# Two normalisations of a fused two-layer block: order of the first product's tiles, place of the weight splits, and the modulation sums

## Reference

```python
# block 1
u = rmsnorm(h, norm_mix)                 # first norm
proj = u @ w_in                          # q, k, v of the delta rule first
...
h = h + square(relu(rmsnorm(h, norm_mlp) @ w_up)) @ w_down
gate = sigmoid(rmsnorm(h, norm_ple) @ w_ple_gate)
h = rmsnorm(h + gate * (p @ w_ple_proj), norm_final)
# block 2
mod = silu(c) @ w_ada + b_ada            # 6 x 1024 values: shift, scale, gate, twice
x = rmsnorm(h, norm_mix_2) * (1 + scale) + shift      # second norm
q = x @ w_in_2[:, 0:512]                 # query product of the retention
```

## Time and profile before

| | before |
|---|---|
| median of 3 runs | 2023.18 us |
| the profiled execution's own time | 2023.73 us |
| its span, first to last instruction | 2021.9 us |
| PE busy | 1936.7 us (96%) |
| DVE busy | 1340.7 us (66%) |
| ACT busy | 892.1 us (44%) |
| POOL busy | 505.7 us (25%) |
| mean granted clock of TensorE | 0.983 |

### The profile page before, as it was taken

One profiled execution on the slowest core, in us unless ns is written; L12 is line 12 of the kernel. 1 busy time (PEld: TensorE's weight loads), 2 busy tenths in 40 slices (PEclk: granted clock), 3 DMA queues, 4 the chain that ended last, 5 costly groups with the idle time before them and its releaser, 6 DMA issues. The chain is left out here.

```text
span 2021.9 us, 24041 instructions
## 1 busy us (share of the span) xinstructions
PE 1936.7 (96%) x8921; PEld 1572.1 (78%) x8921; DVE 1340.7 (66%) x1421; ACT 892.1 (44%) x973; POOL 505.7 (25%) x266
## 2 busy tenths in 40 slices
PE   7998999999999999999999999999999999999992
PEld 6877887888888878768887787877887888878872
DVE  5538857666674666434036464757988998989994
ACT  2224324322323451232002213226887888878883
POOL 3520014000000003515664453510221222321122
PEclk8999999999999998999999999999999999999996
DMA  5321102656552231243236162333999999999994
GB/s 174 111 63 63 34 23 95 207 178 198 199 170 99 100 106 46 91 167 104 88 100 249 63 240 72 108 137 124 371 364 376 371 374 380 378 383 358 358 346 156
DMA packets 115307, 385.38 MB, mean 191 GB/s; under 512 B 21845, under 2 KB 24196, under 8 KB 88734
## 3 DMA queue, kind: packets, MB, share of 16 engines
q1 hardware_dynamic: 98800, 349.88, 47.8%
q10 hardware_dynamic: 10382, 25.42, 3.9%
q0 software_dynamic: 6048, 9.03, 1.3%
HBM read 353.49 MB, written 43.79 MB: 196 GB/s over the span
## 5 line engine op out<-in xcount | busy, mean ns | idle before, releaser
L2949 DVE TENSOR_TENSOR m_lo<-m_raw,m_hi 128x2048 fp32r<-128x2048 f32 x200 | 448.7, 2285 | 9.2 <-ACT m_hi L2877 8.6
L2877 ACT ACTIVATE m_hi<-m_raw 128x2048 fp32r<-128x2048 f32 x200 | 382.7, 1921 | 103.7 <-DMA m_raw<-in_w_exp_gate_dram 71.7
L264 PE MATMUL ps<-xhi,whi 128*128 128x512 f32 x936 | 375.8, 401 | 11.1 <-DVE xlo L461 5.9
L266 PE MATMUL ps<-xhi,wlo 128*128 128x512 f32 x936 | 366.5, 392 | 0.0
L265 PE MATMUL ps<-xlo,whi 128*128 128x512 f32 x936 | 366.3, 391 | 0.0
L241 POOL TENSOR_SCALAR whi<-raw 128x2048 fp32r<-128x2048 f32 (+1 forms) x55 | 104.2, 1894 | 851.6 <-PE ps L266 786.5
L243 POOL TENSOR_TENSOR wlo<-raw,whi 128x2048 fp32r<-128x2048 f32 (+1 forms) x55 | 254.5, 4628 | 4.6
L264 PE MATMUL ps<-m_hi,xt_hi 128*128 128x512 f32 x544 | 217.0, 399 | 8.6 <-DVE xt_lo L2954 7.1
L264 PEld LDWEIGHTS ps<-xhi,whi 128*128 128x128 f32 x936 | 177.0, 189 | 53.4 <-issue 14.2
L265 PE MATMUL ps<-m_lo,xt_hi 128*128 128x512 f32 x544 | 213.9, 393 | 0.0
L266 PE MATMUL ps<-m_hi,xt_lo 128*128 128x512 f32 x544 | 212.9, 391 | 0.0
(11 more groups left out here) (476 smaller groups left out, 2999.5 us busy)
## 6 DMA issues: line engine op xcount, KB each, us to landing
m_raw<-in_w_exp_gate_dram SPq DMA_DIRECT2D x68, 1024.0 KB, 6.3
m_raw<-in_w_exp_up_dram SPq DMA_DIRECT2D x68, 1024.0 KB, 6.6
m_raw<-in_w_exp_down_dram SPq DMA_DIRECT2D x68, 1024.0 KB, 6.4
raw<-in_w_in_dram SPq DMA_DIRECT2D x42, 1024.0 KB, 5.2
ada_w<-in_w_ada_dram ACTq DMA_DIRECT2D x48, 512.0 KB, 4.2
y_rows<-xhi SPq DMA_DIRECT2D x39, 512.0 KB, 10.6
raw<-in_w_up_dram SPq DMA_DIRECT2D x16, 1024.0 KB, 5.7
raw<-in_w_down_dram SPq DMA_DIRECT2D x16, 1024.0 KB, 5.1
```

The costliest lines, as they stand in the source:

```text
L264: nc.tensor.matmul(o, lh, rh, start=start, stop=False)
L266: return nc.tensor.matmul(o, ll, rh, start=False, stop=stop)
L2877: nc.scalar.activation(m_hi[s][:], m_raw[s][:], ACT.Copy).then_inc(m_split, 1)
L2949: nc.vector.tensor_tensor(m_lo[s][:], m_raw[s][:], m_hi[s][:].bitcast(F32), ALU.subtract).then_inc(m_low, 1)
```

## The change

- `linear` gets `by_tile`: the first chunk of a unit goes tile by tile, each tile into all four banks before the next tile. It is used for the first unit of the kernel, the first MLP unit and the query unit.
- First norm: GpSimd makes the high part of chunk 0 in quarters of 512 columns, VectorE its low quarters between the tiles of the norm, and TensorE waits for each quarter by itself. Chunk 1's high part goes from GpSimd to ScalarE, behind the third tile.
- Modulation: in MLP units 12 and 13 VectorE transposes `ada_acc` in 32x32 blocks and reduces each block row, six parts of 1024 columns; a matrix `pick` is made once. Four products in `gate_sums` finish all 48 sums. `mod_out` moves into the first gate half, and a bank of the second projection waits for it.
- Second norm: TensorE takes the squares' sum from three operands as they come, with 23 unread products between, and no sums in the query product. ScalarE loads its table ahead of the last square, and the high part of the query unit's second chunk stands behind the third tile of the norm; VectorE's low part of the first chunk moves from ahead of the second gate half to behind it, that of the second chunk to k = 5.
- GpSimd waits for those two splits before it goes on with its own chunks.

```diff
@@ def linear
-                pe.wait_ge(split_done, n + 1)
+                if parts is None or k0:
+                    pe.wait_ge(split_done, n + 1)
...
+                if by_tile and k0 == 0:
+                    for k in range(rows):
+                        if parts is not None and k < rows - 1:
+                            pe.wait_ge(parts, k + 1)
+                        elif parts is not None:
+                            pe.wait_ge(split_done, n + 1)
+                        if ready is not None and ready[1] + k >= 0:
+                            pe.wait_ge(ready[0], ready[1] + k + 1)
+                        for m in range(4):
...
+                            last = three(bank(u, m), wh[:, k, c], wl[:, k, c], hi[:, k, :], lo[:, k, :], k == 0, False)
+                    last.then_inc(chunk_used, 1)
@@ def scale_tiles
-                if k >= 1:
+                if early_low is not None and k < 3:
+                    early_low(k)
+                    low(k)
+                elif k >= 1 and not (early_low is not None and k == 3):
                     low(k - 1)
@@ def high_tiles
             for k in range(KT):
+                if k == 3 and after is not None:
+                    after()
@@ sums of the modulation
-        def mod_sums(pe, acc, j0, n, b):
-            for j in range(j0, j0 + n):
-                last = nc.tensor.matmul(ps[:, b, j:j + 1], acc[:, j * P:j * P + P], ones[:, 0:1], start=True, stop=True)
-            return last
+        def fold_part(dve, part):
...
+            nc.vector.transpose(fold_t[:], ada_acc[:, part * D:part * D + D]).then_inc(fold_turn, 1)
+            dve.wait_ge(fold_turn, part + 1)
+            nc.vector.tensor_reduce(fold[:, part * S32:part * S32 + S32], fold_t[:].rearrange("p (c q) -> p c q", q=S32),
+                                    AX, ALU.add).then_inc(fold_sum, 1)
...
+        def mod_sums(pe, b):
+            pe.wait_ge(fold_sum, 6)
+            pe.wait_ge(pick_made, 1)
+            by_quarter = fold[:].rearrange("p (j q) -> p q j", q=P // S32)
+            for q in range(P // S32):
+                at = P - S32 - S32 * q
+                last = nc.tensor.matmul(ps[:, b, 0:6 * KT], pick[:, at:at + P], by_quarter[:, q], start=q == 0, stop=q == P // S32 - 1)
+            last.then_inc(mod_full, 1)
@@ GpSimd
-                for n in range(PAIR):
-                    pool.wait_ge(raw_full[n % RAW], 16)
-                    nc.gpsimd.tensor_scalar(whi[:, n, :], raw[:, n % RAW, :], 1.0, 1.0, ALU.mult, ALU.mult).then_inc(split_hi, 1)
+                pool.wait_ge(raw_full[0], 16)
+                for k in range(4):
+                    c = slice(k * T, k * T + T)
+                    ins = nc.gpsimd.tensor_scalar(whi[:, 0, c], raw[:, 0, c], 1.0, 1.0, ALU.mult, ALU.mult)
+                    ins.then_inc(*((first_hi, 1) if k < 3 else (split_hi, 1)))
...
+                pool.wait_ge(split_done, ple_end + 2)
@@ TensorE
+                        linear(pe, u, (xhi, xlo), ready=(x_ready, 0), by_tile=True, parts=first_lo)
...
+                            linear(pe, u, (yhi, ylo), ready=(gain_ready, 0), between=square_sums, by_tile=True)
...
+                    pe.wait_ge(lin_free[side(u)], 4 * nth(u) + 2)
+                    mod_sums(pe, 4 * side(u) + 1)
...
-                    linear(pe, U_proj[i], (p_hi, p_lo))
+                    linear(pe, U_proj[i], (p_hi, p_lo), free={1: (mod_done, 2)} if i else None)
...
-                sums_between(0, 16, a + 1).then_inc(mod_full, 1)
-                mean_squares(pe, 3, a)
...
-                sums_between(16, 12, 4 * side(g) + 1)
...
-                linear(pe, U_rq, (xhi, xlo), ready=(x_ready, 8), gaps=late_sums)
+                for _ in range(5):
+                    unread()
+                pe.wait_ge(nrm_add, 6 * 3 - 1)
+                nc.tensor.matmul(ps[:, a, :], ones, norm_acc[:], start=True, stop=False).then_inc(nrm_add, 1)
+                pe.wait_ge(nrm_sq, 8 * 3 - 1)
+                nc.tensor.matmul(ps[:, a, :], ones, norm_sq[:, 0, :], start=False, stop=False)
+                for _ in range(2):
+                    unread()
+                pe.wait_ge(nrm_sq, 8 * 3)
+                nc.tensor.matmul(ps[:, a, :], ones, norm_sq[:, 1, :], start=False, stop=True).then_inc(nrm_sum, 1)
+                for _ in range(16):
+                    unread()
+                linear(pe, U_rq, (xhi, xlo), ready=(x_ready, 8), by_tile=True)
@@ ScalarE
-                high_tiles(act, 0)
+                high_tiles(act, 0, after=second_chunk)
...
+                    if i:
+                        nc.scalar.preload_act_table_set(LOG_EXP)
                     squares(act, 3, lambda k: (ple_mul, k + 1), [4 * i + 3], both_col)
-                nc.scalar.preload_act_table_set(LOG_EXP)
-                chunk_high(act, ple_end + 1)
                 roots(act, 3, 4 * side(U_proj[1]), eps2_col)
-                high_tiles(act, 1, mod[:, 0:8])
+                high_tiles(act, 1, mod[:, 0:8], after=lambda: chunk_high(act, ple_end + 1))
@@ VectorE
-                chunk_low(dve, 0)
+                first_low(0)
...
+                        if 4 * i + m in range(ADA, ADA + 6):
+                            fold_part(dve, 4 * i + m - ADA)
+                        elif 4 * i + m == ADA + 6:
+                            pick_make(dve)
...
+                        mod_out(dve, 1, 0, 16, at[:, 0:16], (8, v_mix2))
...
+                        mod_out(dve, 2, 16, 32, at[:, 16:48])
...
-                    else:
-                        chunk_low(dve, ple_end)
...
-                add_squares(dve, 3, KT - 2)
-                chunk_low(dve, ple_end + 1)
-                mod_out(dve, 1, 0, 16, ps[:, 4 * side(U_proj[1]) + 1, 0:16], (8, v_mix2))
...
-                scale_tiles(dve, mod[:, 8:16], mod[:, 0:8])
-                mod_out(dve, 2, 16, 32, ps[:, 4 * side(U_gate[1]) + 1, 16:48])
+                chunk_low(dve, ple_end)
+                dve.wait_ge(mod_used, 3)
                 dve.wait_ge(nrm_root, 4)
+                scale_tiles(dve, mod[:, 8:16], mod[:, 0:8], halfway=lambda: chunk_low(dve, ple_end + 1))
```

More of the change, by code:

```diff
@@ L275, in bank, with linear @@
             return ps[:, 4 * side(u) + m, :]
-        def linear(pe, u, a, feature_major=True, ready=None, between=None, inside=(), only=None, free=None, gaps=None):
+        def linear(pe, u, a, feature_major=True, ready=None, between=None, inside=(), only=None, free=None, by_tile=False, parts=None):
             hi, lo = a
@@ L289, in linear @@
                     continue
-                pe.wait_ge(split_done, n + 1)
+                if parts is None or k0:
+                    pe.wait_ge(split_done, n + 1)
                 wh = whi[:, n % PAIR, 0:rows * cols].rearrange("p (k n) -> p k n", n=cols)
                 wl = wlo[:, n % PAIR, 0:rows * cols].rearrange("p (k n) -> p k n", n=cols)
+                if by_tile and k0 == 0:
+                    assert feature_major and n != mine[-1] and not inside
+                    for k in range(rows):
[6 more added lines that the diff above has]
+                        for m in range(4):
+                            c = slice(m * P, m * P + P)
+                            if k == 0 and nth(u) >= 1:
+                                pe.wait_ge(lin_free[side(u)], 4 * nth(u) - 3 + m)
+                            if k == 0 and free is not None and m in free:
+                                pe.wait_ge(*free[m])
+                            last = three(bank(u, m), wh[:, k, c], wl[:, k, c], hi[:, k, :], lo[:, k, :], k == 0, False)
+                    last.then_inc(chunk_used, 1)
+                    if between is not None:
+                        between()
+                    k0 += rows
+                    continue
                 for m in range(4):
@@ L300, in linear @@
                         kk = k0 + k
-                        if gaps is not None and m == 0:
-                            gaps(kk)
                         if ready is not None and m == 0 and ready[1] + kk >= 0:
@@ L450, in roots, with scale_tiles @@
             nc.scalar.activation(norm_r[:], norm_r[:], ACT.Exp, scale=-0.5).then_inc(nrm_root, 1)
-        def scale_tiles(dve, gain, shift=None, halfway=None):
+        def scale_tiles(dve, gain, shift=None, halfway=None, early_low=None):
             at = 8 * n_split[0]
@@ L884, in _ @@
                 for i, u in enumerate(U_dn):
-                    linear(pe, u, (xhi, xlo), ready=(x_ready, 0) if i == 0 else None)
+                    if i == 0:
+                        linear(pe, u, (xhi, xlo), ready=(x_ready, 0), by_tile=True, parts=first_lo)
+                    else:
+                        linear(pe, u, (xhi, xlo))
                 linear(pe, U_aq, (xhi, xlo))
@@ L1410, in _ @@
                         act.wait_ge(p_turned, 1)
+                        act.wait_ge(fold_sum, 6)
                         nc.scalar.activation(p_hi[:], ps[:, 4 * side(LAST[0]):4 * side(LAST[0]) + 2, :], ACT.Copy).then_inc(p_split, 1)
```

(7 more changed lines are left out.)

49 lines of the change are left out of this document (26 added, 23 removed).

## The result

The changed kernel's median is 2004.49 us (four runs, 2003.83 to 2007.48). The ratio to the kernel before is 0.9895, 95% interval 0.9868 to 0.9922: against 2023.18 that is 2001.9 us, between 1996.5 and 2007.4. The two medians alone are 18.7 us apart, and 2004.49 would lie just inside the range: the miss is small beside the interval. The profiled execution took 2004.88, its span is 2003.1, and the mean granted clock rose from 0.983 to 0.989.

What follows compares the result with a forecast made beforehand. TensorE bounds the kernel, idling for `xlo` before both norms' products and then running at half clock. Gains 3.1 + 4.5 + 10.4 less losses 0.5, 1.0 and 0.5 make 16.0 us: 2007.2 us, range 2003.8 to 2013.8.

Steps and rivals of the forecast that it cites:

- The second norm's start: Second norm, up to its first product: that product comes at 751.7 before other terms, gain 4.5 us.
- The query product: Product behind the second norm: without small sums between its products and at full clock, gain 10.4 us.
- The sums in the gate stage: Four fp32 products joining `gate_sums`: 1.0 us lost, between 0.4 and 4.1.
- Rotation: Rotary work on VectorE after the second norm: ends near 805, before TensorE wants the banks at 810.6; no cost.
- The folds: Transposes and reductions on VectorE, four of six parts in MLP unit 12: 0.5 us lost, between 0 and 5.2.
- The clash on the last tile: Second norm's last tile may meet GpSimd's next split, which excludes VectorE: 0.5 us lost, between 0 and 1.1.
- The first norm: Kernel start: first product at 18.95 instead of 21.68, chunk ends at 31.56 instead of 34.67; gain 3.1 us.
- no stall, no clash, sums at 0.4 and no half clock at the start: Best case setting the range's low end: 3.2 us less than the forecast, 2004.0 us.
- Cold query product: Rival: query product starts at half clock; 1.6 us lost (2008.8) or 6.4 (2013.6); chance 0.10.
- Slow transposes: Rival: VectorE's transposes take 2.38 us each, 4.6 us more, 2011.8; chance 0.12.
- The start gives nothing: Rival: first norm gains nothing if GpSimd's quarters take turns badly with VectorE; 2010.3 us, chance 0.03.
- The bank change: Slower rival: changing bank every three products keeps the clock low in chunks taken by tile; 31.3 us, 2038.5; chance 0.04.

Runs made afterwards that it cites:

- no_unread: The changed kernel without the 16 products whose result nothing reads, ahead of the query product; median 2009.88 us, ratio 0.9902.
- double_transpose: The changed kernel with each of the six block transposes on VectorE done twice; median 2014.62 us, ratio 0.9944.
- start_only: The kernel before with only the change's first-norm part; median 2023.94 us, ratio 0.9995.

## Why the prediction was right, and where it was wrong

**Right.** TensorE's idle time for `xlo` was what the two norms cost, and the change took it as said. The product started at 18.85 (18.95 forecast) and at 749.49 (750.1). The second norm's start gained 4.47 (4.5): 6.75 at the product less the 2.28 by which everything was early behind the sums. The query product gained 10.61 (10.4). The sums in the gate stage cost 0.89 (1.0). Rotation began at 782.10 and TensorE waited for none of it.

**The terms that were mis-sized.** *The folds*: forecast 0.5 lost, measured 0; the transpose was right (1.24 for 1.22), but the loop's step was 3.73, not 3.86. *The clash on the last tile*: forecast 0.5 lost, measured 0. *The first norm*: forecast 3.1, measured 2.54, 3.47 and 1.83 in three traces, 3.3 in the mean; the step "If the half clock lasts 3.28 us as in the earlier trace rows" took one trace's length for a property of the kernel, while it lasted for 8 to 14 products by trace. With 3.3 at the start and 14.1 from B to C the change is worth 17.4 by the traces, not 16.0: 2005.8, which is inside the range.

**The step that failed** is the range. Its low end counted "no stall, no clash, sums at 0.4 and no half clock at the start", bounds of the change's own terms, as if the stages that the change does not touch stood still. They don't: A to B spans 248 to 257 us in three traces of the changed kernel, and D to end 623 to 632 in all seventeen, whose code there is the same. Of the first trace's 18.8 us of shorter span 17.49 were there at D, and 1.4 came from the expert stage, whose mean is 629.2 over the five traces with the old second norm and 628.6 over the twelve with the new: chance. The three runs from 2022.25 to 2023.19 gave no hint of it; 29 further runs of the kernel before went from 2016 to 2036.

**What stays between the terms and the measured ratio.** The 3.9 us between 17.4 and the 21.3 of the ratio (2023.18 to 2001.9) belong to no step of the change in the traces. Nor do all runs together show them: the 80 runs of the kernel before average 2024.7, the 17 of the changed kernel 2006.6, which is 18.2 apart and, by their scatter of 5.2 and 4.9, known to about 2.6 (an estimate that takes the chips together). The ratio of the changed kernel came out at 0.9895, 0.9893 and 0.9939; that the first lies below the range is not shown to be more than the luck of its four runs. The forecast's "About 0.2%, 4 us" for what a measurement can tell was too fine as well: the interval is 5.4 us each way.

**The rivals.** *Cold query product*: the clock stayed at 1.00; no_unread shows what it would have cost, 1.4, near the lower of its two prices. *Slow transposes*: 1.24 against the 2.38 bound. double_transpose says that the stall would have come, with the clock's fall behind it. The 2.49 estimated from the Trainium skill, "VectorE: DVE Perf Modes", section "The three transpose paths", took eight times the page's figure for one 128x128 bf16 transpose; this one wide fp32 transpose took half of that, so the multiplication didn't hold. *The start gives nothing*: the nine traces with the new start and nothing added to it reach A 1.83 to 3.52 before the first trace's 35.08, but start_only's median can't tell that from nothing. *The bank change*: behind the half clock of the start, the products taken by tile had slots of 0.23 at clock 1.00, with TensorE busy throughout (17.00 of 17.00 us from 754 to 771). The Trainium skill, "TensorE: Matmul & The Clock Gate", section "A second HAM failure mode: psum-queue depth-cycling", tells of an engine that idles briefly between its groups of products, so it doesn't describe this kernel.

**Open:** whether the change is worth 16 or 18 us in the mean run; 18.2 give or take 2.6 holds both. Why one wait lowers the clock in one run and not in the next wasn't settled, nor what makes the expert stage vary by 9 us.

## What to carry to other kernels

Before a sum is made, profile the kernel before twice and cut both traces at the same instructions: what differs between them belongs into the range, whatever the change does. A wait of TensorE can cost more than its own length, by half clock behind it, but its length alone doesn't say so: among the heads the clock fell behind the wait of 2.04 us in all thirteen unfilled traces and behind that of 1.22 us in seven, while behind one of 1.69 us in the retention (889.67 in the kernel before) it fell in none of seventeen. So look at the granted clock behind a wait before you fill it; the fill was worth 1.4 us ahead of the query product, where TensorE paces what follows, and little where ScalarE or a transfer does. An engine that is released earlier (GpSimd here) may start its next long pass just when the critical engine still needs the memory; order it by a wait (7.30 us became 1.48).

## What was not expected of the hardware

- The same wait lowers the clock or not, by run: 1.22 us near 207 did nothing in one trace and brought some 10 us at half clock in another; after the start's idle time 8 to 14 products ran at half clock.
- Two VectorE operations of 0.69 us took 7.30 beside GpSimd's two passes of 2.37 and 4.83.
- VectorE's block transpose of 128x1024 fp32 takes 1.24 us, the time of a reduction of the same size (1.22).
